# A two-layer recurrent block on one Trainium2 core: loads released buffer by buffer in the RWKV core, and attention whose bias, maximum and normalisation are joined into other operations

## The reference, cut to what matters

```python
def step(S, inp):
    r_t, w_t, k_t, v_t, a_t, b_t = inp
    sa = jnp.einsum('bhvk,bhk->bhv', S, a_t)
    S = S * w_t[:, :, None, :] + sa[..., None] * b_t[:, :, None, :] + v_t[..., None] * k_t[:, :, None, :]
    y = jnp.einsum('bhvk,bhk->bhv', S, r_t)
    return S, y
```

```python
scores = jnp.einsum('bnqkgd,bnskd->bnkgqs', qb, kb) * scale
scores = jnp.where(mask, scores + bias, -jnp.inf)
m = jnp.maximum(jnp.max(scores, axis=-1, keepdims=True), sink)
e = jnp.exp(scores - m)
probs = e / (jnp.sum(e, axis=-1, keepdims=True) + jnp.exp(sink - m))
out = jnp.einsum('bnkgqs,bnskd->bnqkgd', probs, vb)
```

## Time and profile before

| | before |
|---|---|
| median of 3 runs | 4240.87 us |
| the three runs | 4235.71, 4240.87 and 4574.26 us |
| profiled execution, its own time | 4235.85 us |
| span of that execution | 4234.0 us |
| PE busy | 3694.1 us, 87% |
| DVE busy | 1735.5 us, 41% |
| ACT busy | 1003.7 us, 24% |
| POOL busy | 1336.2 us, 32% |

### The profile page before, as it was taken

The page is one execution under the profiler, slowest core; times in us unless marked ns, Lnnn a source line. Parts: engine busy times, 40 slices in busy tenths (PEclk is TensorE's granted clock), DMA queues, the critical chain, the costliest instruction groups (busy, mean ns, idle before and its releaser), DMA issues. The chain is left out here.

```text
span 4234.0 us, 62397 instructions
## 1 busy us (share of the span) xinstructions
PE 3694.1 (87%) x26724; PEld 2945.4 (70%) x26724; DVE 1735.5 (41%) x1747; ACT 1003.7 (24%) x1119; POOL 1336.2 (32%) x989
## 2 busy tenths in 40 slices
PE   5997999999998679967777879999999989857788
PEld 4775788888876467756676757888888777753567
DVE  5554331221344621126676633313223444287552
ACT  3552110000022622224444412101001220131221
POOL 1442233333332122223333322333333313374242
PEclk9998999999999789989999989999999999878999
DMA  2111111111110222221212021111111102100211
GB/s 80 45 41 38 35 49 45 46 48 45 45 56 29 104 85 82 86 93 35 72 38 73 23 80 40 45 50 45 50 45 44 59 26 89 46 1 1 75 45 65
DMA packets 59365, 221.82 MB, mean 52 GB/s; under 512 B 6576, under 2 KB 6833, under 8 KB 58673
## 3 DMA queue, kind: packets, MB, share of 16 engines
q1 hardware_dynamic: 49968, 185.57, 12.8%
q10 hardware_dynamic: 9216, 33.56, 2.0%
HBM read 181.36 MB, written 37.75 MB: 52 GB/s over the span
## 5 line engine op out<-in xcount | busy, mean ns | idle before, releaser
L141 PE MATMUL ps<-xh,whi 128*128 128x512 f32 x4160 | 1340.6, 404 | 194.4 <-DVE xl L343 51.8
L141 PE MATMUL ps<-xl,whi 128*128 128x512 f32 x4160 | 1327.7, 401 | 0.0
L141 PE MATMUL ps<-xh,wlo 128*128 128x512 f32 x4160 | 1326.8, 400 | 0.0
L141 PEld LDWEIGHTS ps<-xh,whi 128*128 128x128 f32 x4160 | 793.0, 192 | 414.1 <-issue 141.4
L141 PEld LDWEIGHTS ps<-xl,whi 128*128 128x128 f32 x4160 | 795.2, 191 | 194.0
L141 PEld LDWEIGHTS ps<-xh,wlo 128*128 128x128 f32 x4160 | 794.8, 191 | 193.9
L115 POOL TENSOR_TENSOR gap<-ones 128x1 f32<-128x1 f32 x258 | 69.2, 268 | 2346.5 <-PE ps L141 2265.8
L118 POOL TENSOR_TENSOR wlo<-wraw,whi 128x1024 fp32r<-128x1024 f32 (+3 forms) x258 | 644.8, 2499 | 21.5
L116 POOL TENSOR_SCALAR whi<-wraw 128x1024 fp32r<-128x1024 f32 (+3 forms) x258 | 285.8, 1108 | 0.0
L572 DVE TENSOR_TENSOR h<-ps,h 128x1024 f32 x56 | 68.6, 1225 | 423.2 <-PE ps L141 423.2
L644 ACT ACTIVATE sq<-sq 128x1024 f32<-128x1024 f32 x44 | 46.7, 1061 | 775.6 <-DVE sq L658 775.6
(11 more groups left out here) (392 smaller groups left out, 3660.5 us busy)
## 6 DMA issues: line engine op xcount, KB each, us to landing
wraw<-w_ffn_in SPq DMA_DIRECT2D x88, 512.0 KB, 3.2
rw_kept<-rw_stage ACTq DMA_DIRECT2D x48, 512.0 KB, 2.6
rw_next<-rw_kept SPq DMA_DIRECT2D x40, 512.0 KB, 5.8
wraw<-w_ffn_out SPq DMA_DIRECT2D x32, 512.0 KB, 3.2
wraw<-w_ple SPq DMA_DIRECT2D x16, 640.0 KB, 4.0
wraw<-w_b_in SPq DMA_DIRECT2D x18, 512.0 KB, 3.2
wraw<-w_hawk_in SPq DMA_DIRECT2D x10, 640.0 KB, 3.9
wraw<-w_ffn_out SPq DMA_DIRECT2D x16, 384.0 KB, 3.0
```

The costliest lines, as they stand in the source:

```text
L141: last = nc.tensor.matmul(acc[:, hf, :], w[:, s, c:c + P], x[:, kt, hf * HALF:(hf + 1) * HALF], start=start and kt == 0 and n == 0, stop=s ...
```

## The change

In the RWKV core the five loads of the next pair no longer wait together for `gram_ak` of the pair at work. `sw`, `kx` and `a` wait for `hat_go`, `r` for `prep_ready`, `v` for the eighth `tr_done`. All of them still stand ahead of the store and the gate in SP's queue.

In attention the bias table is multiplied by 8 on the host side. `maximum` does per head one `tensor_tensor_reduce`, which computes (scores + bias) times 1/8 and the maximum of it and the sink; it replaces lines 2004, 2006 and 2007. The sum of the exponentials comes out of the exponentials themselves (`accum_out`), so line 2015 goes. The probabilities are no longer divided on DVE: `normalise` writes into a new tile `diag` the identity times the reciprocal sum, one 128x128 block per head, and PE multiplies the exponentials by that block instead of transposing them with the identity. Since `diag` has one buffer, `normalise(n)` waits for the product of block n - 1.

```diff
@@ rw_core, block.sync
                 def load(m):
-                    for n, buf in ((RW_W, sw), (RW_K, kx), (RW_A, a), (RW_R, r), (RW_V, v)):
+                    if m:
+                        sp.wait_ge(g.hat_go.sem, g.hat_go.base + m)
+                    for n, buf in ((RW_W, sw), (RW_K, kx), (RW_A, a)):
                         sp.dma_start(buf, g.rw_tile[n][m]).then_inc(g.rw_loaded.sem, 16)
+                    if m:
+                        sp.wait_ge(g.prep_ready.sem, g.prep_ready.base + m)
+                    sp.dma_start(r, g.rw_tile[RW_R][m]).then_inc(g.rw_loaded.sem, 16)
+                    if m:
+                        sp.wait_ge(g.tr_done.sem, g.tr_done.base + NT * m)
+                    sp.dma_start(v, g.rw_tile[RW_V][m]).then_inc(g.rw_loaded.sem, 16)
...
                     if m + 1 < KD:
-                        sp.wait_ge(g.gram_ak.sem, g.gram_ak.base + m + 1)
                         load(m + 1)
@@ bias_constants
-    return out
+    return out * np.float32(HD ** 0.5)
@@ attention, block.tensor
-                                last = nc.tensor.transpose(g.ps[:, 4 + h // 2, (h % 2 * 2 + kb) * P:(h % 2 * 2 + kb + 1) * P],
-                                                           score[:, n % 2, h, kb * P:(kb + 1) * P], g.ident[:])
+                                last = nc.tensor.matmul(g.ps[:, 4 + h // 2, (h % 2 * 2 + kb) * P:(h % 2 * 2 + kb + 1) * P],
+                                                        score[:, n % 2, h, kb * P:(kb + 1) * P], diag[:, h, :], start=True, stop=True)
@@ attention, exponentials
-                        ins = nc.scalar.activation(score[:, n % 2, h, k0:], score[:, n % 2, h, k0:], ACT.Exp, bias=neg_mx[:, n % 2, h:h + 1])
+                        ins = nc.scalar.activation(score[:, n % 2, h, k0:], score[:, n % 2, h, k0:], ACT.Exp, bias=neg_mx[:, n % 2, h:h + 1],
+                                                   accum_out=rs[:, n % 2, h:h + 1])
@@ attention, maximum
-                    nc.vector.scalar_tensor_tensor(sc, src, HD ** -0.5, bias[:, :, k0:], ALU.mult, ALU.add).then_inc(g.sc_read.sem, 1)
+                    for h in range(NH):
+                        ins = nc.vector.tensor_tensor_reduce(sc[:, h], src[:, h], bias[:, h, k0:], HD ** -0.5, sinks[:, h:h + 1], ALU.add, ALU.max, mx[:, b, h:h + 1])
+                    ins.then_inc(g.sc_read.sem, 1)
                     dve.wait_ge(g.sc_read.sem, B(g.sc_read, n + 1))
-                    ch.link(dve, nc.vector.tensor_reduce(mx[:, b, :], sc, AXX, ALU.max))
-                    ch.link(dve, nc.vector.tensor_tensor(mx[:, b, :], mx[:, b, :], sinks, ALU.max))
@@ attention, normalise
-                    ch.link(dve, nc.vector.tensor_reduce(rs[:, b, :], sc, AXX, ALU.add))
                     ch.link(dve, nc.vector.tensor_tensor(rs[:, b, :], rs[:, b, :], es[:, b, :], ALU.add))
                     ch.link(dve, nc.vector.reciprocal(rs[:, b, :], rs[:, b, :]))
-                    nc.vector.tensor_tensor(sc, sc, wide(rs[:, b, :], WIN - k0), ALU.mult).then_inc(g.prob_ready.sem, 1)
+                    eye = g.ident[:].rearrange("p (o q) -> p o q", o=1).broadcast_to([P, NH, P])
+                    if n:
+                        dve.wait_ge(g.pt_done.sem, B(g.pt_done, n))
+                    nc.vector.tensor_tensor(diag[:], eye, wide(rs[:, b, :], P), ALU.mult).then_inc(g.prob_ready.sem, 1)
```

More of the change, by code:

```diff
@@ L1865, in attention @@
         vtok = sb("at_vtok", [P, NT, P])
+        diag = sb("at_diag", [P, NH, P])
         mx, neg_mx, es, rs = (sb(f"at_{n}", [P, 2, NH]) for n in ("mx", "neg_mx", "es", "rs"))
@@ L2011, in normalise @@
                 def normalise(n):
-                    k0, b = 0 if n else P, n % 2
-                    sc = score[:, b, :, k0:]
+                    b = n % 2
                     dve.wait_ge(g.e_ready.sem, B(g.e_ready, n + 1))
-                    ch.link(dve, nc.vector.tensor_reduce(rs[:, b, :], sc, AXX, ALU.add))
                     ch.link(dve, nc.vector.tensor_tensor(rs[:, b, :], rs[:, b, :], es[:, b, :], ALU.add))
                     ch.link(dve, nc.vector.reciprocal(rs[:, b, :], rs[:, b, :]))
-                    nc.vector.tensor_tensor(sc, sc, wide(rs[:, b, :], WIN - k0), ALU.mult).then_inc(g.prob_ready.sem, 1)
+                    eye = g.ident[:].rearrange("p (o q) -> p o q", o=1).broadcast_to([P, NH, P])
+                    if n:
+                        dve.wait_ge(g.pt_done.sem, B(g.pt_done, n))
+                    nc.vector.tensor_tensor(diag[:], eye, wide(rs[:, b, :], P), ALU.mult).then_inc(g.prob_ready.sem, 1)
                 maximum(0)
```

## The result

| | before | after |
|---|---|---|
| median of 6 runs | 4246.0 us | 4220.16 us |
| ratio of the undisturbed runs | | 0.9946, 95% interval 0.9931 to 0.9961 |
| profiled execution, its own time | 4235.85 us | 4226.95 us |
| RWKV core, from the first issue of its queue to the last gate | 580.3 us | 587.7 us |
| attention, as SP waits through it | 149.1 us | 133.5 us |

(The 4574.26 us of the kernel before is a disturbed run; the ratio leaves it out.) The change makes the kernel 0.54% faster, about 23 us, where 39 were forecast. Attention gave what was forecast of it, 15.6 us. The core gave nothing, although the wait that should pay for it is gone.

The account below looks back on a forecast made before the run. The prediction took both stages as bound by engine-to-engine chains: DVE's load wait in the core, DVE's work in attention's later blocks. 4235.85 - 24 (core) - 15 (attention) = 4197 us, range 4180 to 4223.

Parts of the forecast that it names:

- 15 us were forecast: Attention: 15 us gained, taken between POOL's 14 and 18, with bounds of 0 and 19 us.
- Rival (e): Attention: each result read waits for its piece and blocks the next, 2.5 us a pair; slower, 4262 us; chance 0.03.
- Rival (a): Attention gives nothing back, PE's longer products running at the low clock, 19 us a block; 4212 us; chance 0.15.
- the 11.8 us: Attention: PE's row of a block without S5's part, copy, AV, scores and products at full clock, sets the block.
- the POOL bound: End of attention: beyond 14 us gained POOL holds the stage, less about 4 us its own operations save.
- The wait goes whole: Core: DVE's 33.6 us idle before decay_sum in loops 0 to 6 vanishes, as loads land before DVE asks.
- so these three loads go out some 23 us earlier than now: Core: the loads of sw, kx and a leave right behind line 1528, some 23 us earlier.
- nothing waits: Core: store and gate held some 6 us behind v delay nobody; cost 0, uncovered 6 us in 6 loops.
- so I price the meeting at 0 to 1 us in each of 7 loops and set it against the clock: Core: early loads meeting PE's solutions and outputs cost 0 to 1 us a loop, offset by PE keeping its clock.
- Sum: 33.6 - 5 x 0.3 - 2.0 - 5.9: Core: the wait less what PE's first inverse still holds in the loops, 24 us gained, bounds 15 and 31.
- Rival (b): Core: early loads starve PE's instructions, one fetch a loop waiting 2.5 us, core gains 6 us; 4215 us; chance 0.11.
- Rival (d): Core: nothing moves, the chain is held elsewhere and DVE's wait becomes one for PE; 4233 us; chance 0.05.

Follow-up runs that it names:

- attention alone: Against the kernel before, the whole of attention's edit with the core's load queue left as it was; 4220.33 us, ratio 0.9956.
- by-time: Against the full change, loads for pair m + 2, with sw, kx, a ahead of store and gate, r and v behind; 4218.72 us, ratio 0.9947.
- core only: Against the kernel before, only the core's new load queue, with attention unchanged; 4235.85 us, ratio 0.9993.
- decay first: Against the full change, core loads back at gram_ak, the decay table's load with its own signal for decay_sum; 4200.64 us, ratio 0.9910.
- no loads: Against the full change, the core's loads of pairs 1 to 7 left out, so it works on stale inputs; 4192.73 us, ratio 0.9891.

## Why the prediction was right and wrong

**Attention: right in size.** 15 us were forecast and 15.6 came in this profile. The five other kernels with the whole of attention's change have stages of 128.2 to 132.0 us, 17 to 21 below 149.1, and the runs of attention alone say 19 (11 to 25). The rows of the kernel after that answer to the earlier trace rows:

```profile
3751.24 0.48 DVE L2014 CUSTOM_DVE_ANT_0 at_score<-ps,at_bias,vectors 128x256 f32<-128x256 f32 x1 [8.29 <-PE ps L1925]
3751.65 0.08 DVE L2014 DVE_READ_ACCUMULATOR2_ANT at_mx<- 128x1 f32 x1
3751.65 0.48 DVE L2014 CUSTOM_DVE_ANT_0 at_score<-ps,at_bias,vectors 128x256 f32<-128x256 f32 x1
...
3755.18 1.23 DVE L2028 TENSOR_TENSOR at_diag<-ident,at_rs 128x1024 f32<-128x1024 f32 x1
...
3759.35 0.50 ACT L1971 ACTIVATE at_score<-at_score,at_neg_mx 128x256 f32<-128x256 f32 x1
3759.75 0.19 ACT L1971 ACTIVATION_READ_ACCUMULATOR at_score<-at_score,at_neg_mx 128x1 f32 x1
3759.84 0.49 ACT L1971 ACTIVATE at_score<-at_score,at_neg_mx 128x256 f32<-128x256 f32 x1
...
3762.30 3.84 PE L1925 MATMUL ps<-at_diag,at_score 128*128 128x128 f32 x32
```

- A pair takes 0.40 us from start to start (0.5 taken, 0.27 to 0.60 bounded). The read is 0.08 us and lies beside the next piece. Rival (e), 2.5 us a pair, is out. Cutting did cost time: eight pieces take 3.3 us, where one pass over 2048 elements took 2.29. It paid because they replace two passes and a small operation, 4.8 us. The estimate of 392 ns a piece from the Trainium skill (VectorE: DVE Perf Modes, the TRN2 errata) meets the 0.40 us.
- The diagonal took 1.23 us as forecast where POOL let it. Its mean over the eight is 2.06 us (16.5 / 8).
- ACT's exponentials go from 0.40 to 0.49 us a head, inside the bound, and ended before they were asked for.
- PE's 16 products take 3.84 us at the full clock (3.5 forecast). The Trainium skill's factor of four (TensorE: Matmul & The Clock Gate, Terms) would need the old transpositions' 1.97 us to become 7.9; the trace disagrees with it. Rival (a), an attention that gives nothing back, is out by the 15.6 us, though the clock it feared is there in part (0.82 in the stage, not 1.0).
- The blocks are longer than the 11.8 us: the products start at 3762.30, 3775.91, 3789.50, 3801.74 and 3811.72, that is 13.6, 13.6, 12.2 and 10.0 us apart, at a clock of 0.83 to 0.92 until 3800. And POOL does not hold the end, as I said it would:

```profile
3815.06 2.35 POOL L2222 TENSOR_TENSOR s_turn<-s_turn,sum_of_squares 128x1024 f32<-128x1024 f32 x1
...
3820.76 2.02 PE L1958 MATMUL ps<-h,s_bbar 128*32 128x128 f32 x64
```

POOL ends at 3817.41 and PE at 3822.78, 5.4 us later. The size was right because longer blocks took the place of the POOL bound, not by the reason given. That is luck.

**The core: wrong.** 24 us were forecast, about 3 came. "The wait goes whole" was right: 33.6 to 0.0 us. Three steps failed; the second decided.

1. "so these three loads go out some 23 us earlier than now". They stand behind the store of pair m - 1, and that one waits for the end of loop m. I wrote of the new queue that "nothing waits" and asked only who needs the store, never what stands behind it. The loads left 5 us earlier instead. The by-time kernel shows that this alone did not cost the gain.
2. "so I price the meeting at 0 to 1 us in each of 7 loops and set it against the clock". This is the step that decided. Ahead of the grams PE idles 12.6 us more than before (35.0 - 22.4), some 2 us a loop, and 2.2 more in the outputs. Nor did the clock stand against it: it was 0.90 in the core (0.92 with core only), where 0.92 stood before, and in loop 3 a gap of 3.66 us is followed by 64 products in 3.68 instead of 2.08 us. The rows of 1.43, 1.92 and 1.65 us from which I priced it had loads beside some and none beside others, and I read that as no effect. They were different places in the code; only the same place with and without loads can be compared.
3. "Sum: 33.6 - 5 x 0.3 - 2.0 - 5.9", the 24 us. The sum takes DVE's work as unchanged once it no longer waits. Even with decay first, where no load meets the grams, PE's idle time for the steps fell by 13.8 us. In the full change it fell by 11.2, and by 3.3 in the inverses. `decay_sum` itself took 10 us more (29.6 for 19.6), which no term held; it explains the missing 1.0 us of loop 3. How the rest divides over the other loops stays open.

Rival (b), 0.11, has this mechanism at 2.5 us a loop and with 4215 nearly this size: 21 us below 4235.85, where the runs show 23. It was right but for the place, grams instead of outputs, and by-time shows the outputs too. Its chance was too small. Rival (d), a core that gives nothing because the chain is held elsewhere, is out as a mechanism, since decay first won by the wait; its 4233 also leaves out attention's 15 us.

**What stays open.** How much of decay first's gain is the clock's is known only as 6 to 15 us. The grams keep 11 us of gaps without any load; whether another length or place of the code removes these was not tried. Nor was the release of the last four loads behind the first inverses, which could win at most the 8 us between decay first and no loads.

## What to carry to other kernels

When a wait for loads is to go, first ask whether the waiter needs all of them: a signal of its own for the one load that is needed first won 20 us without moving a byte, while moving the loads earlier won the same wait and lost it to the engine beside which they now ran. Price a moved transfer by what runs in the place it moves to, by comparing the same place with and without traffic. And in a queue, trace each new wait in both directions: who needs what stands behind it, and what its own predecessor is waiting for.

## What the runs showed of the hardware

- Instructions come in packets of some 0.02 MB through the DMA engines that carry the data, and a packet beside five bulk transfers came 2.8 to 4.5 us later than one without (3.9 and 5.6 against 1.1). 30 spare transfers made this kernel some 20 us longer in that way.
- A longer gap can cost twice. In the kernel after, the 64 products behind gaps of 2.25 to 4.39 us took 3.68 us each time. Behind shorter gaps both are found: before, 2.08 us behind 0.91 but 3.49 behind 0.87, and with attention alone 3.20 behind 0.91.
- The first of five loads issued together lands early enough to be used: with its own signal DVE's wait in loops 0 to 6 went from 33.6 to 2.0 us:

```profile
L1486 DVE TENSOR_TENSOR_SCAN rw_next<-wraw,rw_next 128x256 f32<-128x256 uint8 x28 | 30.0, 1073 | 2.0 <-DMA rw_next<-rw_kept 2.0
```

- Once DVE no longer waits, its `decay_sum` runs beside an operation of POOL and takes twice as long. Timeline of the kernel after, POOL and DVE:

```profile
2116.89 2.88 POOL L1227 TENSOR_TENSOR rw_levels<-rw_levels,rw_masks 128x512 f32<-128x512 f32 x2 [14.82 <-PE ps L1308]
...
2117.35 1.35 DVE L1492 TENSOR_TENSOR_SCAN rw_next<-wraw,rw_next 128x256 f32<-128x256 uint8 x1
...
2121.81 0.67 DVE L1492 TENSOR_TENSOR_SCAN rw_next<-wraw,rw_next 128x256 f32<-128x256 uint8 x1
```

  The group grew from 19.6 to 29.6 us, which no term of the forecast held.
- Two kernels with the same code in a stage of 580 us differed there by up to 7 us in single profiles, and three others by 10 (560.2, 559.8 and 569.8). One per cent of a stage is not to be read from one profile each.
